# Two-block transformer kernel: mixing stage with two joined weight blocks, half-array products, and the result stored by chunk

## The reference

```python
h = rms_norm_2(x, mix_norm[l])
(aq, ak, av, iq, ik, iw, mx, mv, mi, mf, mo, ga, gb) = split_columns(h @ w_in[l])
...                                       # q, k and ik are normalised per head of 64 features
ya = dsa_attention(q, k, v, iq, ik, iw)   # 8 query heads, 2 key heads, 64 features each
yb = mlstm_branch(mx, mv, mi, mf, mo, ...)  # 4 heads, q and k of 64, v of 128 features
merged = sigmoid(ga) * (ya @ w_proj_a[l]) + sigmoid(gb) * (yb @ w_proj_b[l])
x = x + merged @ w_out[l]
```

## The kernel before

| slot | PE | others |
|---|---|---|
| 6 to 9 | index logits (`idx_logits`, 20 units) | ACT relu, DVE weighted sum (`idx_add`), DVE convolution (`conv`) |
| 10 to 27 | | DVE selection of the best 128 keys (`select`): 16 rounds for each of three query blocks, in 6 slots each |
| 11 + 3h | `head_qk` of mLSTM head h | ACT copies q and k into `m_qk` |
| 12 + 3h | `head_max`, `head_scores` | ACT exp (`head_decay`), DVE `head_weight` |
| 13 + 3h | `head_num` | ACT squares, DVE `head_scale` |
| 14 + 3h | | ACT `out_root`, DVE `head_out` (writes `m_h`) |
| 15 + 3h | `head_turn` | DVE `head_gate`, ACT `out_high`; one slot later DVE `head_low` |
| 25 + u | `att_scores` of unit u (two query heads, one block of 128 queries; 16 units) | DVE `att_max`, ACT `att_exp` |
| 26 + u | `att_turn` (transposes) | ACT `att_turned` |
| 27 + u | `att_out` | ACT `att_scaled`; every fourth unit PE `att_join`, ACT `att_high`, DVE `att_low` |

## Time and profile before

### The profile page before, as it was taken

One profiled execution on the slowest core, in us unless ns is written; L12 is line 12 of the kernel. 1 busy time (PEld: TensorE's weight loads), 2 busy tenths in 40 slices (PEclk: granted clock), 3 DMA queues, 4 the chain that ended last, 5 costly groups with the idle time before them and its releaser, 6 DMA issues.

```text
span 2593.7 us, 31934 instructions
## 1 busy us (share of the span) xinstructions
PE 2544.2 (98%) x11624; PEld 2078.6 (80%) x11624; DVE 1323.2 (51%) x1666; ACT 941.5 (36%) x1230; POOL 99.9 (4%) x86
## 2 busy tenths in 40 slices
PE   7999999999999999999999999999999998999998
PEld 5888788888777788888888888888778876888887
DVE  6445543444555655544345445446779435544343
ACT  5566442233223333432234322224453452322222
POOL 1000100001000000100003000002000000000000
PEclk9999999999999999999999999999999999999999
DMA  2211232333222222333332233323212212223333
GB/s 100 64 57 49 88 94 95 97 96 121 90 74 73 73 89 81 103 97 97 96 95 94 96 97 97 97 96 107 66 57 65 66 57 81 91 96 97 97 97 105
DMA packets 62776, 226.38 MB, mean 87 GB/s; under 512 B 6768, under 2 KB 6768, under 8 KB 62576
## 3 DMA queue, kind: packets, MB, share of 16 engines
q1 hardware_dynamic: 62704, 225.39, 27.4%
HBM read 223.26 MB, written 2.10 MB: 87 GB/s over the span
## 4 chain that ended last, share of the span: by engine, by line
PE 96%; DVE 2%; ACT 1%; DMA 0%; issue 0%; SPq 0%; ACTq 0%; DVEq 0%
PE ps L1666 55%; PE ps L1669 27%; PE ps L2138 2%; PE ps L1766 2%; PE ps L1879 1%; PE ps L1711 1%; PE ps L1780 1%; PE ps L2082 1%; PE ps L1868 1%; PE ps L2108 1%; PE ps L1748 1%; PE ps L1980 1%; PE ps L1704 1%; PE ps L1698 0%; PE ps L1701 0%; PE ps L1793 0%
## 5 line engine op out<-in xcount | busy, mean ns | idle before, releaser
L454 ACT ACTIVATE w_hi<-raw 128x1024 fp32r<-128x1024 f32 x417 | 442.5, 1061 | 1324.1 <-PE ps L1669 1282.1
L1666 PE MATMUL ps<-x_hi,w_hi 128*128 128x512 f32 x2064 | 820.2, 397 | 0.0
L1666 PE MATMUL ps<-x_lo,w_hi 128*128 128x512 f32 x2064 | 806.2, 391 | 0.0
L950 DVE TENSOR_TENSOR w_lo<-raw,w_hi 128x1024 fp32r<-128x1024 f32 x417 | 512.9, 1230 | 154.1 <-ACT w_hi L454 153.7
L1669 PE MATMUL ps<-x_hi,w_lo 128*128 128x512 f32 x2064 | 509.8, 389 | 0.0
L1666 PEld LDWEIGHTS ps<-x_hi,w_hi 128*128 128x128 f32 x2064 | 388.9, 188 | 84.6 <-issue 4.3
L1666 PEld LDWEIGHTS ps<-x_lo,w_hi 128*128 128x128 f32 x2064 | 388.9, 188 | 84.6 <-issue 4.3
L1669 PEld LDWEIGHTS ps<-x_hi,w_lo 128*128 128x128 f32 x2064 | 387.4, 188 | 80.5
L1666 PE MATMUL ps<-u_hi,w_hi 128*128 128x512 f32 x864 | 336.1, 389 | 0.0
L1666 PE MATMUL ps<-u_lo,w_hi 128*128 128x512 f32 x864 | 336.1, 389 | 0.0
L1060 DVE SCALAR_TENSOR_TENSOR h<-ps,h 128x512 f32 (+1 forms) x136 | 94.1, 692 | 344.5 <-PE ps L1669 343.3
(11 more groups left out here) (307 smaller groups left out, 2223.3 us busy)
## 6 DMA issues: line engine op xcount, KB each, us to landing
raw<-in_stream SPq DMA_DIRECT2D x417, 512.0 KB, 3.5
x_tok<-in_x SPq DMA_DIRECT2D x1, 2048.0 KB, 7.5
out_x<-x_tok SPq DMA_DIRECT2D x1, 2048.0 KB, 6.6
tab_ret<-in_tables_ret SPq DMA_DIRECT2D x1, 1536.0 KB, 6.5
tab_mix<-in_tables_mix SPq DMA_DIRECT2D x1, 384.0 KB, 3.8
prm<-in_params SPq DMA_DIRECT2D x1, 302.5 KB, 7.9
tab<-in_tables SPq DMA_DIRECT2D x1, 256.0 KB, 7.7
```

Source lines behind the costliest of these rows:

```text
L454: nc.scalar.activation(w_hi[:, slot(n)], raw[:, slot(n)], ACT.Copy).then_inc(hi_done, 1)
L950: nc.vector.tensor_tensor(w_lo[:, slot(n)], raw[:, slot(n)], w_hi[:, slot(n)].bitcast(F32), ALU.subtract).then_inc(lo_done, 1)
L1666: nc.tensor.matmul(ps[:, gemm_bank(n)], w_hi[:, s, k], x(k), start=(k == 0 and i == 0), stop=False)
```

## The change

It does ten things.

1. **Joined blocks.** "G" and "IK" become one block "IKG", the two "K" blocks become one block "KK". The stream in memory is unchanged; SP gathers the columns with three and two DMAs (`part`). `MIX_ORDER` has 39 entries. Mixing work moves up accordingly (logits and heads by one slot, attention by two).
2. **Keys by halves.** `ik_n` holds the index keys in both halves of the partitions, without padding. `k_n` holds each key head in both halves; the second copy is made by ACT (`key_twice`). Index logits, `head_scores` and `att_scores` contract 64 rows, alternately in the lower and the upper half of the array.
3. **`head_qk`** is one product for q and k together; ACT then makes four copies (q and k, each in both halves) where it made two.
4. **`head_max`** takes high and low gate rows in one product (`g_rows`).
5. **`att_out`** has values as the stationary operand (64 columns) and probabilities as the moving one, and writes the transposed output, one head to each half of the columns. `att_join`, `att_scaled` and `o_q` go. The division by the softmax sum moves to DVE (`att_sum`), ahead of `att_turn`; `att_sum` now stands at the head of a slot.
6. **`query_means`** is four products in quarters of the columns, then a copy by ACT and four transposes (`query_turn`), where it was 16 products.
7. **Selection** of each query block takes 8 slots with 2 rounds each, from slot 9 on. Index logits have 10 units in slots 5 to 9, in two pairs of banks where they had four banks.
8. **`head_low`** moves from DVE to POOL.
9. **Seams.** The second half of the first projection block, not the first, waits for the last `att_max`. The first two blocks of `w_out` are interleaved (`of_merged`), so that they start on six of the eight chunks of `merged`.
10. **The end.** After each of the last eight blocks PE transposes the chunk before it (`out_turn`), ACT copies it and issues a store of 256 KB (`out_chunk`).

```diff
-MIX_ORDER = ([("G", 0), ("IK", 0)] + [("IQ", c) for c in range(4)] + [("MX", c) for c in range(4)] +
-             [(name, c) for c in range(4) for name in ("MV", "MO")] + [("K", 0), ("K", 1)] +
+MIX_ORDER = ([("IKG", 0)] + [("IQ", c) for c in range(4)] + [("MX", c) for c in range(4)] +
+             [(name, c) for c in range(4) for name in ("MV", "MO")] + [("KK", 0)] +
...
-TOPK_FROM, TOPK_SLOTS, TOPK_ROUNDS = 10, 6, (0, 3, 6, 9, 12, 14, 16)
-HEAD_FROM, HEAD_EVERY = 11, 3
+TOPK_FROM, TOPK_SLOTS, TOPK_ROUNDS = 9, 8, (0, 2, 4, 6, 8, 10, 12, 14, 16)
+HEAD_FROM, HEAD_EVERY = 10, 3
...
+            def load_keys_and_gates(n):
+
+                sp.wait_ge(lo_done, n + 1)
+                index, gate = RUN_AT["mix"] + MIX_STREAM["IK"], RUN_AT["mix"] + MIX_STREAM["G"]
+                part(n, 0, index, 0, IDX_DIM).then_inc(sig("parts_in"), 16)
+                part(n, 64, gate, 32, 56).then_inc(sig("parts_in"), 16)
+                part(n, GATE_IW, gate, 0, IDX_HEADS).then_inc(raw_full[n % 2], 16)
...
             def head_qk(h):
 
                 act.wait_ge(sig("mqk_done"), h + 1)
-                nc.scalar.activation(m_qk[0:ML_QK, 0], ps[0:ML_QK, 0], ACT.Copy, scale=ML_QK ** -0.5).then_inc(sig("mq_moved"), 1)
-                nc.scalar.activation(m_qk[0:ML_QK, 1], ps[0:ML_QK, 1], ACT.Copy).then_inc(sig("mq_moved"), 1)
+                low, high = slice(0, ML_QK), slice(ML_QK, P)
+                for rows in (low, high):
+                    nc.scalar.activation(m_qk[rows, 0], ps[low, 0], ACT.Copy, scale=ML_QK ** -0.5).then_inc(sig("mq_moved"), 1)
+                    nc.scalar.activation(m_qk[rows, 1], ps[high, 0], ACT.Copy).then_inc(sig("mq_moved"), 1)
...
             def att_sum(u):
 
+                seen = (u // 4 + 1) * P
                 dve.wait_ge(sig("aexp_done"), 2 * u + 2)
                 nc.vector.reciprocal(stat[:, 3, 2 * u:2 * u + 2], stat[:, 2, 2 * u:2 * u + 2]).then_inc(sig("ainv_done"), 1)
+                step("ainv_done", u + 1)
+                for i in range(2):
+                    row = s_m[:, u % 2, i, 0:seen]
+                    nc.vector.tensor_scalar(row, row, stat[:, 3, 2 * u + i:2 * u + i + 1], None, ALU.mult).then_inc(
+                        sig("ascale_done"), 1)
...
                 for i in range(2):
-                    last = nc.tensor.matmul(ps[:, i, 0:seen], aq[:, c, tb * P:(tb + 1) * P], k_pad[:, i, c // 2, 0:seen],
+                    rows = slice(i * ATT_DIM, (i + 1) * ATT_DIM)
+                    last = nc.tensor.matmul(ps[:, i, 0:seen], aq[rows, c, tb * P:(tb + 1) * P], k_n[rows, c // 2, 0:seen],
                                             start=True, stop=True, skip_group_check=True)
...
+                for kb in range(tb + 1):
+                    for i in range(2):
+                        rows = slice(i * ATT_DIM, (i + 1) * ATT_DIM)
+                        last = nc.tensor.matmul(ps[rows, 4 + tb % 2, c * P:(c + 1) * P],
+                                                a_v[:, kb, c // 2 * ATT_DIM:(c // 2 + 1) * ATT_DIM],
+                                                p_t[:, u % 2, i, kb * P:(kb + 1) * P], start=(kb == 0), stop=(kb == tb),
+                                                skip_group_check=True)
...
-            pe.wait_ge(sig("mg_lo_done"), DC)
-            run(RUN_AT["w_out"], DC, lambda k: mg_hi[:, k], lambda k: mg_lo[:, k])
+            of_merged(first, (0, 1, 2, 3, 4, 5))
+            of_merged(first + 1, (0, 1))
+            of_merged(first, (6, 7))
+            of_merged(first + 1, (2, 3, 4, 5, 6, 7))
```

More of the change, by code:

```diff
@@ L320, in build @@
         p_t = sb("p_t", [P, 2, 2, T])
-        k_pad = sb("k_pad", [P, 2, ATT_KV, T])
+        k_n = sb("k_n", [P, ATT_KV, T])
         aq = sb("aq", [P, 4, T])
@@ L561, in two @@
                     split_hi(later(n, 3))
-                pairs(act, first, blocks - 2 if first + blocks == N_BLOCKS else blocks, two)
+                pairs(act, first, blocks, two)
             def ahead_of_norm(first, k):
@@ L614, in groups @@
                         ahead_of_norm(n, next_norm)
+                    elif g == len(sizes):
+                        for c in range(DC):
+                            if c + 2 < DC:
+                                split_hi(n + c + 2)
+                            if c:
+                                out_chunk(c - 1)
+                        out_chunk(DC - 1)
                     elif g >= 1:
@@ L918, in _ @@
                     att_exp(unit_at(s, 0))
-                if unit_at(s, 3) is not None and unit_at(s, 3) % 4 == 3:
-                    att_high(unit_at(s, 3) // 4)
                 if s == MIX_SLOTS:
@@ L1403, in idx_add @@
                 dve.wait_ge(sig("irelu_done"), i + 1)
-                for k in range(heads):
-                    hd, part = first + k, ps[:, i % 4, k * seen:(k + 1) * seen]
+                for k in range(2 * heads):
+                    hd, part = first + k, ps[:, i % 2 * 2 + k % 2, k // 2 * seen:(k // 2 + 1) * seen]
                     weight = iw[:, tb, hd:hd + 1]
@@ L1549, in _ @@
             for s in range(MIX_SLOTS + DC):
+                if unit_at(s, 1) is not None:
+                    att_sum(unit_at(s, 1))
                 if s == 0:
@@ L1639, in _ @@
                     mix_constants()
+                    for h in range(ML_HEADS):
+                        head_low(h)
                 if k == N_FINAL:
@@ L2184, in _, with of_merged, out_turn @@
                     att_scores(unit_at(s, 0))
-            pe.wait_ge(sig("mg_lo_done"), DC)
-            run(RUN_AT["w_out"], DC, lambda k: mg_hi[:, k], lambda k: mg_lo[:, k])
-            groups(FFN_GROUPS, RUN_AT["ffn2"], 2 * HIDDEN // P + D_FF // P, 2, N_FFN2)
-            moved(N_BLOCKS - 2)
-            moved(N_BLOCKS - 1)
-            for i in range(2 * TB):
-                if i >= 4:
-                    pe.wait_ge(sig("out_ready"), i - 3)
-                for q in range(4):
-                    last = turn_block(ps[:, i % 4, q * P:(q + 1) * P], h[:, i % 2 * 4 + q, i // 2 * P:(i // 2 + 1) * P])
-                last.then_inc(sig("out_turned"), 1)
+            def of_merged(n, chunks):
+                if chunks[0] == 0:
+                    pe.wait_ge(lo_done, n + 3)
+                    pe.wait_ge(bank_free[slot(n)], turn(n, 1))
+                pe.wait_ge(sig("mg_lo_done"), chunks[-1] + 1)
+                for k in chunks:
+                    for i, (w, x) in enumerate(((w_hi, mg_hi), (w_hi, mg_lo), (w_lo, mg_hi))):
+                        last = nc.tensor.matmul(ps[:, GEMM_BANK + slot(n)], w[:, slot(n), k], x[:, k], start=(k == 0 and i == 0),
+                                                stop=(k == DC - 1 and i == 2), skip_group_check=True)
+                if chunks[-1] == DC - 1:
+                    last.then_inc(mm_done, 1)
+            first = RUN_AT["w_out"]
+            of_merged(first, (0, 1, 2, 3, 4, 5))
+            of_merged(first + 1, (0, 1))
+            of_merged(first, (6, 7))
+            of_merged(first + 1, (2, 3, 4, 5, 6, 7))
+            run(first + 2, DC - 2, lambda k: mg_hi[:, k], lambda k: mg_lo[:, k])
+            def out_turn(c):
+                moved(N_RUN - DC + c)
+                if c >= 2:
+                    pe.wait_ge(sig("out_ready"), c - 1)
+                for b in range(TB):
+                    last = turn_block(ps[:, c % 2, b * P:(b + 1) * P], h[:, c, b * P:(b + 1) * P])
+                last.then_inc(sig("out_turned"), 1)
+            groups(FFN_GROUPS, RUN_AT["ffn2"], 2 * HIDDEN // P + D_FF // P, 2, N_FFN2)
 def weight_block(w, rows, cols):
```

361 lines of the change are left out of this document (193 added, 168 removed).

## The result

The changed kernel takes 2539.99 us, the median of 4 runs (2538.15 to 2540.18); the kernel before, run beside it, 2596.16 (2592.46 to 2597.64). The ratio is 0.9781, 95% interval 0.9769 to 0.9792: faster. The forecast was 2534.4, its range 2524 to 2553. The profiled execution has an own time of 2540.18 us and a span of 2538.4, 55.3 less than before where 61.1 were forecast.

The account below looks back on a forecast made before the run. PE's own queue was taken as the bound. Queue 39.6 + waits going 16.2 + clock 8.5 - new waits 7.0 + end 3.8 = 61.1 us off the 2593.7 span gives 2532.6, plus 1.8 is 2534.4 us; range 2524 to 2553.

Parts of the forecast that it names:

- forecast case: Whole kernel: all terms as summed, 2534.4 us, own range 2527 to 2542; chance 0.56.
- The queue, 39.6 net: PE's queue: 50.1 us of work taken out, less 10.5 us for changes between whole and halved array.
- the 70 changes: Logits, head_scores, query_means, attention slots: 70 changes between whole and halved array at 0.15 us, 10.5 us; bounds 3.5 and 17.5.
- Waits that go, 16.2: Mixing stage: all seven waits of PE, 5.4 to 1.0 us long, go, together 16.2 us.
- Waits that come, 7.0: New PE waits: slot 14 2.3 us, first attention slot 1.5, next nine 2, small ones 1.2; together 7.0, bounds 2 and 14.
- The clock, 8.5: Mixing stage: the lower clock behind the three long waits goes with them, giving back 8.5 us.
- ACT and DVE give back more: Rival: slot 14's wait draws the lower clock (5.1 us) and other waits double (7): 2546.5 us; chance 0.20.
- The end, 3.8: From last product's end to span's end: 12.6 us becomes 5.8, seven transpose groups add 3.0 to the queue; saved 3.8.
- Short rows: Loads of "IKG" and "KK" in short rows, 0.02 us a row: "IKG" takes 6 us of some 8.5, costing nothing.
- Slower: Rival: each short row costs 0.36 us, so "IKG" is 63 us late and "KK" 36: 2633 us; chance 0.02.
- IKG lands late: Rival: the "IKG" load lands 9 us late and the clock loses 5.1: 2548.5 us; chance 0.08.
- float32 row halves run one after the other: Rival, index logits, head_scores and att_scores: 7.9 + 3.5 + 8.8 us come back, 2554.6 us; chance 0.08.

Follow-up runs that it names:

- experiment 3: Kernel of experiment 2 with DVE doing att_sum between the two rounds of selection of the same slot: 2528.62 us, ratio 0.9734 to the kernel before.
- experiment 5: Changed kernel with index logits, head_scores and att_scores contracting all 128 rows again (wrong results, for time alone): 2547.00 us, ratio 0.9810 to the kernel before.
- Experiment 6: Changed kernel with the first two w_out blocks in plain order, waiting for all eight chunks: 2545.61 us, ratio 0.9802 to the kernel before.
- experiment 10: Kernel of experiment 3 with the first two w_out blocks not interleaved, chunks still awaited in parts: 2530.24 us, ratio 0.9743 to the kernel before.
- experiment 2: Changed kernel with ACT's square root ahead of the head_qk copies and the gates: 2532.63 us, ratio 0.9749 to the kernel before.
- experiment 7: Changed kernel with the end as before the change, one 2 MB store by SP: 2542.32 us, ratio 0.9791 to the kernel before.
- experiment 1: The changed kernel run again, nothing altered: 2538.22 us, ratio 0.9771 to the kernel before.
- experiment 4: Changed kernel with ACT's square root between the two gates, measured in one run: stage 390.4 us, PE waits 2.0 us for m_h.
- experiment 8: Changed kernel with att_out ahead of att_turn in each attention slot, measured in one run: 2538.07 us.
- experiment 9: Kernel of experiment 3 with att_out's products of one head behind each other, not alternating: 2531.93 us, ratio 0.9750 to the kernel before.

## Why the prediction was right, and where it was off

Direction and mechanism held, and the time lies 5.6 us above the forecast, inside the range of 2524 to 2553, and also inside the narrower one of the forecast case, 2527 to 2542. In the span, 5.8 us less were gained than summed. By terms, the stage's 51.9 us against 57.3:

- **The queue, 39.6 net: 37.0 measured.** (51.9, less 16.2 - 6.4 = 9.8 of waits, less 8.5 - 3.4 = 5.1 of clock.) This is a remainder, but the slots bear it out. In the late slot, the rows of `att_scores` and `att_out` are each 0.81 us shorter. What was mis-sized is the price of a change of mode, 0.15 us. A slot with four key blocks took 5.49 + 0.87 + 1.73 + 1.78 = 9.87 us from row start to row start and takes 8.62, 1.25 less. Halving the last two saves 1.75, so three changes cost 0.50 together, 0.17 each; a slot with one key block (6.61, then 6.70 in experiment 3, 0.45 of it halved away) gives 0.18. By 0.18, the 70 changes cost 12.6 us and the queue saves 37.5; the short waits, which cost some 0.2 more than they last, take the other 0.5. The price is not the same for all: by the slot of experiment 5 the column halves with two changes save 9.87 - 9.30 = 0.57 us and not 0.87, so 0.15 a change, and the row halves with one change more save 0.68 and not 0.89, so 0.21. The row halves as a whole, 12.8 and not 15.1 us, are 2.3 of the missing 2.6. The Trainium skill ("TensorEngine Tiling (Array Packing)", Key Properties) has each change drain TensorE; with the run-out of 0.17 us as the drain that rule gave 11.9 us, nearer to the measured cost than my 10.5.
- **Waits that go, 16.2: right** to the last one. Experiment 6 shows the largest, and that it hung on how the first two blocks of `w_out` wait; experiment 10, that the waiting by chunk did most of it and the interleaving the rest.
- **Waits that come, 7.0: 6.4 measured.** Slot 14 was forecast at 2.3 us and is 2.5, for the reason given: experiment 2 took the copies and gates from ahead of the square root, and it went. The first attention slot was forecast at 1.5 and is 1.5. The "next nine" gave 0.8 and not 2, and the small ones 1.6 and not 1.2.
- **The clock, 8.5: 5.1 measured.** This is the step that failed: "with the three long waits the clock's 8.5 us go" put at nothing that the new wait of 2.3 us could draw the lower clock. The rival "ACT and DVE give back more" had it, at 5.1 us; 3.4 came in the profile, and by the other runs with that wait it is 0 to 3.4, so the size of this term is in part chance. That rival's other half, waits doubled to 14 us, did not come.
- **The end, 3.8: 4.4 measured**, 4.3 in experiment 7. From the end of the last product's row, 2533.1, it is 5.3 us to the span's end, where 5.8 were forecast; a store of 256 KB landed in 2.3 us, where I had taken 3.
- **Short rows: cost nothing, as forecast.** The three DMAs of "IKG" and a plain load, between 1765 and 1795 us (size, issue to landing):

```profile
raw<-in_stream SPq DMA_DIRECT2D x6, 512.0 KB, 3.5
raw<-in_stream SPq DMA_DIRECT2D x1, 256.0 KB, 3.2
raw<-in_stream SPq DMA_DIRECT2D x1, 224.0 KB, 3.7
raw<-in_stream SPq DMA_DIRECT2D x1, 32.0 KB, 3.4
```

  They need no longer than whole blocks. The price of 0.02 us that I took for a short row was right: in the trace the packets of these DMAs took 18, 16 and 9 ns for 256, 224 and 32 bytes, against the 360 of the rival "Slower". The upper bound was read from a wrong row: the second row is of 2102 to 2120 us, 18 us and not 16, and gives 0.09 us for 2 KB, not 0.08; nothing hangs on it. The rivals "IKG lands late" and "Slower" fell here; PE has no wait for `w_hi` in the stage. The Trainium skill ("DMA: Bandwidth & Descriptors", Specifications) sets a read-modify-write below 512 bytes; a penalty large enough to matter does not show in these rows of 256, 224 and 32 bytes.
- **The rival "float32 row halves run one after the other"** fell in experiment 5.

That adds up: 2.6 us less from the queue, 3.4 from the clock, 0.6 more from waits and 0.6 more at the end, and 1.0 in the part ahead, which experiment 1 shows to be the execution's: 61.1 - 2.6 - 3.4 + 0.6 + 0.6 - 1.0 = 55.3.

## What to carry to other kernels

Where PE is the bound, half-size float32 products in two halves of the array are worth nearly half their time if they alternate; count 0.14 to 0.21 us for each change between whole, row-halved and column-halved array, and write the loops so that no half gets more than two products in a row. A wait of PE can cost more than it lasts: behind those of 1.5 us and longer the lower clock took 0 to 3.4 us here, and 5.1 behind one of 2.9 before the change. So an instruction that releases PE (here one square root of 0.3 us) belongs ahead of copies and table loads that nobody waits for yet. Where a consumer needs many late chunks, let it wait chunk by chunk: that took 4.4 of 5.4 us here, and borrowing work from the next block the rest.

## What the runs showed of the hardware that was not expected

- The lower clock behind a wait differs between executions of the same program with the same wait. Behind the wait of 1.5 us for `s_m` it fell in experiments 1, 2 and 7 (0.83 over 10 us in the first two) and stayed at 1.00 in the first profile and in experiments 4, 6 and 8. Ahead of the stage, in code that no edit touches, PE waits 2.6 us for `r_v` in all twelve profiles; the lower clock follows in eleven and not in that of experiment 2. Near the start, the 20 us from 15 have a mean of 0.66 in the first profile of the changed kernel and 0.74 in that of the kernel before, with the same code. The Trainium skill ("TensorE: Matmul & The Clock Gate", Part 1) says that the number of slow products differs from run to run at a kernel's start; here it does behind waits in the middle as well. A sum should carry such a term as a range.
- Two halves overlap over two products even when they are not written alternately: nothing more with two products a head, 0.27 us with three, 0.49 with four (experiment 9).
- A DMA with 1,024 rows of 32 bytes landed within 3.4 us, as loads of 512 KB did (3.5); one such row took 9 ns.
